# Decay products of a scan as two column halves, with the order of its neighbours changed, in a two-block transformer kernel

## The reference

```python
# stick-breaking attention, 8 heads
z = einsum('bqhd,bkhd->bhqk', q, k) * scale
log_keep = where(past, log_sigmoid(-z), 0.0)
between = cumsum(log_keep, axis=3, reverse=True) - log_keep
a = where(past, exp(log_sigmoid(z) + between), 0.0)
# even layer: short convolution, 3 taps, 1024 channels
y_a = sc_b * causal_depthwise_conv(sc_c * sc_v, sc_conv_w) * silu(sc_z)
# time steps of the scan, 32 heads
dt = softplus(ssd_dt + ssd_dt_bias)          # ssd_dt = h @ w_in[:, 9216:9248]
# scan, per chunk of 128 positions, 4 groups of 8 heads, 64 values a head
y_diag = einsum('bcqkg,bcqkgh,bckghp->bcqghp', cb, decay, xdt)
# output of the even layer: 3584 input channels
x = x + concat(y_b, y_mem, y_a) @ w_out
```

## Time and profile before

| | us |
|---|---|
| runs | 2659.9, 2661.48, 2664.15 |
| median | 2661.48 |
| the profiled execution | 2659.44 |
| its span | 2657.8 |
| TensorE busy in the span | 2635.8 (99%) |
| VectorE, ScalarE, GpSimd busy | 1564.2, 1343.3, 339.1 |

### The profile page before, as it was taken

The page is one execution under the profiler, slowest core; times in us unless marked ns, Lnnn a source line. Parts: engine busy times, 40 slices in busy tenths (PEclk is TensorE's granted clock), DMA queues, the critical chain, the costliest instruction groups (busy, mean ns, idle before and its releaser), DMA issues. The chain is left out here.

```text
span 2657.8 us, 35526 instructions
## 1 busy us (share of the span) xinstructions
PE 2635.8 (99%) x12007; PEld 2188.8 (82%) x12007; DVE 1564.2 (59%) x1833; ACT 1343.3 (51%) x1776; POOL 339.1 (13%) x523
## 2 busy tenths in 40 slices
PE   9999999999999999999999999999999999999998
PEld 7888888888888888888888888888888789888887
DVE  6444456667555555555455665446777765556864
ACT  6544455654444444444444554446565445554443
POOL 2100032211110000000000211001110110123400
PEclk9999999999999999999999999999999999999999
DMA  8876676678776767667666887667677777787775
GB/s 311 308 228 219 214 235 217 206 239 273 230 236 215 226 207 225 209 223 227 215 219 210 264 255 232 208 203 240 223 227 228 230 251 225 227 263 230 215 234 162
DMA packets 175720, 611.77 MB, mean 230 GB/s; under 512 B 23184, under 2 KB 26304, under 8 KB 175360
## 3 DMA queue, kind: packets, MB, share of 16 engines
q1 hardware_dynamic: 133632, 485.03, 56.2%
q0 software_dynamic: 37184, 121.07, 15.5%
q10 hardware_dynamic: 4800, 4.26, 0.6%
HBM read 559.36 MB, written 52.47 MB: 230 GB/s over the span
## 5 line engine op out<-in xcount | busy, mean ns | idle before, releaser
L1859 DVE TENSOR_TENSOR w_lo<-raw,w_hi 128x1024 fp32r<-128x1024 f32 x919 | 1116.4, 1222 | 865.2 <-ACT w_hi L1283 858.5
L1283 ACT ACTIVATE w_hi<-raw 128x1024 fp32r<-128x1024 f32 x919 | 963.9, 1058 | 914.7 <-PE acc L830 769.1
L824 PE MATMUL acc<-w_hi,x_t_hi 128*128 128x512 f32 (+1 forms) x2400 | 949.9, 396 | 0.4 <-ACT w_hi L1283 0.4
L824 PE MATMUL acc<-w_hi,x_t_lo 128*128 128x512 f32 (+1 forms) x2400 | 932.9, 389 | 0.0
L830 PE MATMUL acc<-w_lo,x_t_hi 128*128 128x512 f32 (+1 forms) x2400 | 639.9, 388 | 0.6 <-DVE w_lo L1859 0.6
L830 PEld LDWEIGHTS acc<-w_lo,x_t_hi 128*128 128x128 f32 x2400 | 450.5, 188 | 93.2 <-DVE w_lo L1859 1.0
L824 PEld LDWEIGHTS acc<-w_hi,x_t_hi 128*128 128x128 f32 x2400 | 450.9, 188 | 91.8 <-issue 1.9
L824 PEld LDWEIGHTS acc<-w_hi,x_t_lo 128*128 128x128 f32 x2400 | 451.0, 188 | 90.7 <-issue 1.9
L824 PE MATMUL acc<-w_hi,ff_t_hi 128*128 128x512 f32 x352 | 136.9, 389 | 0.0
L824 PE MATMUL acc<-w_hi,ff_t_lo 128*128 128x512 f32 x352 | 136.9, 389 | 0.0
L830 PE MATMUL acc<-w_lo,ff_t_hi 128*128 128x512 f32 x352 | 94.1, 389 | 0.0
(11 more groups left out here) (395 smaller groups left out, 2677.3 us busy)
## 6 DMA issues: line engine op xcount, KB each, us to landing
raw<-stream SPq DMA_DIRECT2D x919, 512.0 KB, 4.3
d_in<-tile POOLq DMA_DIRECT2D x20, 512.0 KB, 3.7
d_ev<-tile POOLq DMA_DIRECT2D x20, 512.0 KB, 4.9
d_x<-tile POOLq DMA_DIRECT2D x16, 512.0 KB, 4.4
r_b<-d_x POOLq DMA_DIRECT2D x64, 128.0 KB, 6.4
xin<-d_x POOLq DMA_DIRECT2D x16, 512.0 KB, 7.7
d_h<-tile POOLq DMA_DIRECT2D x14, 512.0 KB, 5.7
h_b<-d_h POOLq DMA_DIRECT2D x56, 128.0 KB, 4.6
```

The costliest lines, as they stand in the source:

```text
L824: nc.tensor.matmul(out, src[x][:, chunk + c, t * P:(t + 1) * P], w_hi[:, s, w], start=first and c == 0 and x == 0, stop=False)
L1283: nc.scalar.activation(w_hi[:, u.slot, :], raw[:, u.slot, :], ACT.Copy).then_inc(hi_ready, 1)
L1859: nc.vector.tensor_tensor(w_lo[:, s, :], raw[:, s, :], w_hi[:, s, :].bitcast(F32), ALU.subtract).then_inc(lo_ready, 1)
```

## The change

Six edits in one step.

- The decay products of the scan are issued as two halves of 64 stationary columns, at tile positions (0, 0) and (0, 64), each into its own half of the PSUM partitions.
- The time-step weights stand twice in their unit; VectorE turns the second copy into the low part (`split_beside`), so `w_hi` holds high and low parts side by side, 64 columns a chunk. TensorE makes 2 products a chunk. The two transposes become four fp32 products with pieces of the identity that add both halves.
- In the attention loop the third head's logarithm chain (`log_keep`) stands on ScalarE behind the split of position 7, ahead of the block's output.
- The first tap of the short convolution moves from VectorE to ScalarE (position 9j + 6), and the steps of VectorE are spread over positions 9j + 4 to 9j + 13, one a position; `sc_u` is transposed one position sooner, `sc_w` one later.
- EOUT_ORDER becomes units 0 to 9, 10 to 11 and 12 to 13 of blocks 0 and 1 in turn. TensorE waits for the halves at positions 20 and 24; block 0 ends at 25.
- The loop over the last "ein" units on VectorE is written out to place `split_beside`.

```diff
--- before.py
+++ after.py
@@ -32,7 +32,7 @@
 OLW = 448
 L_SCALE = 192 ** -0.5
 
-EOUT_ORDER = [(b, k) for ks in (range(10), range(10, 14)) for b in range(2) for k in ks]
+EOUT_ORDER = [(b, k) for ks in (range(10), range(10, 12), range(12, 14)) for b in range(2) for k in ks]
 TURN_AT = 3
 FIRST = [(b, k) for ks in (range(6), range(6, 8)) for b in range(2) for k in ks]
 FIRST_END = FIRST.index((0, 7))
@@ -201,7 +201,7 @@
         ("e_ac", [P, 32], F32), ("d_end", [P, 32], F32), ("g_ss", [P, 2], F32), ("g_ms", [P, 2], F32),
         ("g_r", [P, 2], F32), ("bm_t", [P, P], F32), ("cbm", [P, TH, P], F32),
         ("zt", [P, TH, NBW], F32), ("yb", [P, TH, NBW], F32))
-    dt_t = place("dt_t", [32, TOK], F32, XT + 10 * K)
+    dt_t = place("dt_t", [64, TOK], F32, XT + 10 * K)
     HG = 8
     SP_ = 64
     dec, u_in, cv, xs, xdt, xde, st = row_of(
@@ -1049,20 +1049,19 @@
         pe.wait_ge(lo_ready, u.times(1, 1 + RING))
         pe.wait_ge(m_lo, 5)
         for c in range(16):
-            w = slice(32 * c, 32 * c + P)
-            x_hi, x_lo = (x3_t[x][:, c, :] for x in range(2))
-            out = ps_y[:, 0:TOK]
-            nc.tensor.matmul(out, w_hi[:, u.slot, w], x_hi, start=c == 0, stop=False)
-            nc.tensor.matmul(out, w_lo[:, u.slot, w], x_hi, start=False, stop=False)
-            mm = nc.tensor.matmul(out, w_hi[:, u.slot, w], x_lo, start=False, stop=c == 15)
+            w = slice(64 * c, 64 * c + 64)
+            for x in range(2):
+                mm = nc.tensor.matmul(ps_y[0:64, 0:TOK], w_hi[:, u.slot, w], x3_t[x][:, c, :],
+                                      start=c == 0 and x == 0, stop=c == 15 and x == 1)
         mm.then_inc(unit_used, 1)
 
         def time_steps(p):
             if p == 1:
                 pe.wait_ge(dt_v, 1)
                 for t in range(TH):
-                    mm = nc.tensor.transpose(ps_y[:, TOK + 32 * t:TOK + 32 * t + 32], dt_t[:, t * P:(t + 1) * P],
-                                             ident[0:32, 0:32])
+                    for part in range(2):
+                        mm = nc.tensor.matmul(ps_y[:, TOK + 32 * t:TOK + 32 * t + 32], dt_t[:, t * P:(t + 1) * P],
+                                              ident[0:64, 32 * part:32 * part + 32], start=part == 0, stop=part == 1)
                 mm.then_inc(pe_once, 1)
             if p == 5:
 
@@ -1113,8 +1112,10 @@
                 for t in range(TH):
                     for h in range(HG):
                         w = slice(h * SP_, (h + 1) * SP_)
-                        nc.tensor.matmul(turn[t][:, w], dec[:, t, h * P:(h + 1) * P], xdt[:, t, w],
-                                         start=True, stop=True)
+                        for half in range(2):
+                            r = slice(half * SP_, (half + 1) * SP_)
+                            nc.tensor.matmul(turn[t][r, w], dec[:, t, h * P + half * SP_:h * P + (half + 1) * SP_],
+                                             xdt[:, t, w], start=True, stop=True, tile_position=(0, half * SP_))
                 pe.wait_ge(turn_lo, 2 * (TURN["sy"] + g) + 2)
                 nc.tensor.matmul(ps_y[:, :], cv[:, 5, P:TOK], st[:, :], start=True, stop=True).then_inc(s_y, 1)
 
@@ -1146,8 +1147,8 @@
             if q == 6:
                 pe.wait_ge(turn_lo, 2 * TURN["x4"] + 2)
                 pe.wait_ge(m_lo, 5)
-            if q in (20, 22):
-                pe.wait_ge(c_lo, q // 2 - 9)
+            if q in (20, 24):
+                pe.wait_ge(c_lo, q // 4 - 4)
             unit(At(U0["eout"] + q), z_t, UCH * k, (B0["eout"] + b) % 2, k == 0, k == 13)
         for b in range(2, 4):
             pe.wait_ge(sums_out, B0["eout"] + b + 1)
@@ -1393,17 +1394,20 @@
                 splits("win", 8, 8 * b, i, 16)
                 scale_out(At(U0["win"] + 8 * b + 7, i, 16), b, At(STORED["win"], i, 1).times(16, 16), 1)
 
+        def log_keep(j, i):
+            J, m = At(j, i, 4), At(j // 2, i, 2)
+            act.wait_ge(at_z, J.times(1, 2))
+            nc.scalar.activation(keep[:, :], z["sb"][:, :], ACT.Abs).then_inc(at_abs, 1)
+            act.wait_ge(at_abs, m.times(1, 1))
+            nc.scalar.activation(keep[:, :], keep[:, :], ACT.Exp, scale=-1.0).then_inc(at_exp0, 1)
+            act.wait_ge(at_exp0, m.times(1, 1))
+            nc.scalar.activation(keep[:, :], keep[:, :], ACT.Ln, bias=1.0).then_inc(at_keep, 1)
+
         def attend(p, i):
             for j in range(4):
                 J, m, s, kind = At(j, i, 4), At(j // 2, i, 2), j % 2, ("sb", "ca")[j % 2]
-                if p == HEAD_AT_UNIT[j] + 1 and kind == "sb":
-
-                    act.wait_ge(at_z, J.times(1, 2))
-                    nc.scalar.activation(keep[:, :], z["sb"][:, :], ACT.Abs).then_inc(at_abs, 1)
-                    act.wait_ge(at_abs, m.times(1, 1))
-                    nc.scalar.activation(keep[:, :], keep[:, :], ACT.Exp, scale=-1.0).then_inc(at_exp0, 1)
-                    act.wait_ge(at_exp0, m.times(1, 1))
-                    nc.scalar.activation(keep[:, :], keep[:, :], ACT.Ln, bias=1.0).then_inc(at_keep, 1)
+                if p == HEAD_AT_UNIT[j] + 1 and kind == "sb" and p != 7:
+                    log_keep(j, i)
                 if p == HEAD_AT_UNIT[j] + 2 and kind == "ca":
                     act.wait_ge(at_max, m.times(1, 1))
                     for x, w in enumerate((slice(0, P), slice(P, H3))):
@@ -1422,6 +1426,8 @@
         with act.Fori(0, 4) as i:
             for b in range(2):
                 splits("win", 8, 96 + 8 * b, i, 16, lambda k: attend(8 * b + k, i))
+                if b == 0:
+                    log_keep(HEAD_AT_UNIT.index(6), i)
                 scale_out(At(U0["win"] + 96 + 8 * b + 7, i, 16), b,
                           At(STORED["win"] + 6, i, 1).times(16, 16), 1)
 
@@ -1684,7 +1690,14 @@
             if k == 9 * j + 5:
                 act.wait_ge(c_u, j + 1)
                 nc.scalar.activation(sc_in[:, :, 2, :], sc_in[:, :, 3, :], ACT.Tanh, scale=0.5).then_inc(c_th, 1)
-            if k == 9 * j + 11:
+            if k == 9 * j + 6:
+                act.wait_ge(c_ut, j + 1)
+                act.wait_ge(c_y, j)
+                for c in range(4):
+                    at = 16 + 4 * j + c
+                    last = nc.scalar.activation(sc_cv[:, c, :], sc_u[:, c, :], ACT.Copy, scale=col2[:, at:at + 1])
+                last.then_inc(c_conv, 1)
+            if k == 9 * j + 12:
                 act.wait_ge(c_y, j + 1)
                 nc.scalar.activation(z_t[0][:, 20 + 4 * j:24 + 4 * j, :].rearrange("p c t -> p (c t)"),
                                      sc_y[:, :], ACT.Copy).then_inc(c_hi, 1)
@@ -1859,6 +1872,12 @@
             nc.vector.tensor_tensor(w_lo[:, s, :], raw[:, s, :], w_hi[:, s, :].bitcast(F32),
                                     ALU.subtract).then_inc(lo_ready, 1)
 
+        def split_beside(u):
+
+            dve.wait_ge(hi_ready, u.times(1, 1))
+            hi, src = (x[:, u.slot, :].rearrange("p (c h n) -> p c h n", h=2, n=32)[:, :, 1, :] for x in (w_hi, raw))
+            nc.vector.tensor_tensor(hi, src, hi.bitcast(F32), ALU.subtract).then_inc(lo_ready, 1)
+
         def splits(stage, units, first, i, per, hook=None):
             for k in range(units):
                 if hook:
@@ -2260,14 +2279,21 @@
                 turn_set(0)
             mem_job(0, At(0, i, 1), k - 6, z_t, At(16, i, 1).times(1))
 
-        for i in range(4):
+        for i in range(3):
             splits("ein", 16, 16, i, 16, lambda k: ein_beside(k, i))
+        for k in range(16):
+            ein_beside(k, 3)
+            u = At(U0["ein"] + 64 + k + LEAD)
+            if u.k == U0["dt"]:
+                split_beside(u)
+            else:
+                split(u)
         split(At(U0["dt"] + LEAD))
 
         def time_steps(p):
             if p == 0:
                 summed(At(U0["dt"]))
-                nc.vector.tensor_copy(dt_t[:, :], ps_y[0:32, 0:TOK]).then_inc(dt_v, 1)
+                nc.vector.tensor_copy(dt_t[:, :], ps_y[0:64, 0:TOK]).then_inc(dt_v, 1)
             if p == 2:
                 dve.wait_ge(pe_once, 2)
                 dve.wait_ge(cc, 3)
@@ -2409,48 +2435,48 @@
         for g in range(4):
             splits("sc", 16, 16 * g, 0, 0, lambda k: sc_beside(k, g))
 
+        def blocks_of(dst, part):
+            return nc.vector.transpose(dst[:, :, :].rearrange("p c (a i) -> p c a i", i=SQ),
+                                       sc_in[:, :, part, :].rearrange("p a (c i) -> p c a i", i=SQ))
+
         def short(k, j):
             if k == 9 * j + 4:
                 dve.wait_ge(c_in, 64 * (j + 1))
                 nc.vector.tensor_tensor(sc_in[:, :, 1, :], sc_in[:, :, 1, :], sc_in[:, :, 2, :], ALU.mult)\
                     .then_inc(c_u, 1)
+            if k == 9 * j + 5:
+                dve.wait_ge(c_u, j + 1)
+                dve.wait_ge(c_y, j)
+                blocks_of(sc_u, 1).then_inc(c_ut, 1)
             if k == 9 * j + 6:
                 dve.wait_ge(c_th, j + 1)
```

(36 more changed lines are left out.)

## The result

| | before | after |
|---|---|---|
| median, us | 2660.9 | 2645.4 |
| runs, us | 2659.9 to 2664.2 | 2642.5 to 2647.9 |
| profiled execution: span, us | 2657.8 | 2646.3 |
| ratio to before, 95% interval | 1 | 0.9937, 0.9924 to 0.9951 |

What follows compares the result with a forecast made beforehand. TensorE was taken as the bound, busy 2635.8 of 2657.8 us. Terms -4.1 - 4.8 + 3.0 - 1.1 + 1.7 = -5.3 us gave a median of 2656.2 us, range 2647.5 to 2666 us.

Steps and rivals of the forecast that it cites:

- logarithm: Attention loop: with the split ahead of the third head's logarithm, TensorE's wait for `p_t` goes, -4.1 us over 4 passes.
- waits in "eout": Short convolution's new steps and order: four TensorE waits worth 5.3 us go, 0.5 us left for raw weights, -4.8 us.
- later sum of block 0: Stage "eout": block 0 ends later, its store-and-load chain keeps its length, TensorE waits for the splits, +3.0 us (0.5 to 4).
- time steps: Time-step weights: 32 products instead of 48, -1.9 us, and four fp32 products for the transposes, +0.8 us; together -1.1 us.
- scan: Decay products: half records step at 0.057 us, tiles one after the other, plus 0.3 us tiling cost a group; +1.7 us.
- (a): Scan: the two column tiles run at once, 2.1 us a group, -5.7 us in place of +1.7, total 2648.8 us; chance 0.30.
- (b): Scan: a half's load takes as long as a whole one, 7.3 us a group, +15.3 us, total 2669.8 us; chance 0.13.
- (c): Scan: a step of 0.085 us from load and product order within a tile, +8.9 us, total 2663.4 us; chance 0.12.
- (d): Stage "eout": block 0's later end costs nothing because the chain shortens, total 2653.2 us; chance 0.42 together with the forecast.
- (e): Attention loop: reordering the logarithm does nothing, total 2660.3 us; chance 0.03.

Runs made afterwards that it cites:

- neighbours on one tile: Changed kernel with the loops around the scan's half products swapped, so neighbouring products share a column tile; 2650.9 us, ratio 0.9960 to the kernel before.
- whole products: Changed kernel with the scan's products undivided again, as before the change; 2651.4 us, ratio 0.9968 to the kernel before.
- four tiles: Changed kernel with each scan product in four column tiles of 32 output rows instead of two of 64; 2642.5 us, ratio 0.9938 to the kernel before.
- the version beyond: Changed kernel with block 0's transposes one unit later and one summed-identity product for the small time-step transposes; 2641.1 us, ratio 0.9930 to the kernel before.

## Why the prediction was wrong, point by point

| part | predicted, us | measured by the trace, us |
|---|---|---|
| logarithm | -4.1 | -4.1 (alone) |
| waits in "eout" | -4.8 | -5.3 |
| later sum of block 0 | +3.0 | +0.4 to +1.3, +0.7 in the changed kernel |
| time steps | -1.1 | -1.3 |
| scan | +1.7 | -5.5 |
| sum | -5.3 | -15.5 |

The four parts alone give ratios of 0.9982, 0.9988, 0.9984 and 0.9981, whose product is 0.9935, against 0.9937 for the whole change. They add up within their intervals, each some 2.5 us to either side; that the parts' sum by the trace and the difference of the medians are both 15.5 us is closer than either is known.

**A reading.** The prediction calls the wait for `p_t` the largest of TensorE's inside the kernel, and so does. The same view has one above it, line 830 waiting for `w_lo`, 3.3 us in 4 times. The sum does not suffer: the two of these four that lie in "eout" (2.4 us) are counted there, and the change does not touch the others.

**The scan: the step that failed.** "I take 0.057 us, load and stream both halved, tiles one after the other." The halves are right: with neighbours on one tile a record steps by 0.058 us. "One after the other" is wrong: two tiles give 0.029 and four 0.014. This one choice is 7.2 of the 10.2 us that I missed. It was rival (a), with 2.1 us a group forecast and (3.52 - 1.36) = 2.16 measured. I argued against it that "records start in order, and each product is two records on the same tile". The second half is true and no hindrance. The first does not hold from tile to tile, as far as the steps tell: split by tile, the changed kernel's starts put a product's two records 58 ns or more apart, with the other tile's record 6 to 7 ns behind each. Whether the engine changes the order or receives it so is not shown. The 0.3 us for going in and out of the tiling holds: 64 x 0.0295 + 0.3 = 2.19. Rivals (b) and (c) fall, since a half's record steps by 0.058 us on its own tile and not by 0.110 or 0.085.
By the Trainium skill, page TensorEngine Tiling (Array Packing), section Tiling Modes, different tiles can load and multiply in parallel; the traces agree, with 6 ns between the starts on two tiles and 58 ns between those on one. I had the rule before me and gave it 0.30 because no row of this kernel showed it. There was no row against it either, and the value that I took was itself no row's.

**The later sum of block 0: right mechanism, wrong size.** The pair of waits came where I said, for `w_lo` and then `w_hi`. The term failed at "Nothing in it gets shorter" and "16.36 us". The time from the store's issue to the transpose of block 0 in the twelve profiles:

| order | steps | chain, us |
|---|---|---|
| old | old (before, scan alone, time steps alone, logarithm alone) | 16.36, 15.82, 16.41, 14.70 |
| old | new (old order in the changed kernel) | 14.36 |
| new | old (order alone) | 13.39 |
| new | new (short convolution and order, after, neighbours on one tile, whole products, four tiles, the version beyond) | 14.32, 13.78, 13.57, 13.65, 14.00, 14.40 |

So the earlier trace rows showed the chain near its long end, and with both edits it is 1.9 us shorter in the mean (15.8 against 13.9). Either edit alone, in one profile each, has a chain as short as with both, so which of them shortens it isn't settled. For the changed kernel 3.0 - (16.36 - 13.78) = 0.4 us, against 0.7 measured. I had written "a microsecond or so" for this and then not taken it. Which transfer gets out of the chain's way was not tried and stays open. Rival (d), that the later sum costs nothing, was nearer than my term.

**The waits in "eout".** 5.3 us was the right size, and all of it goes; the 0.5 us that I left for raw weights was not needed. The mechanism holds: the raw weights are late by 8.66 us with the new order and old steps, and by 3.72 us at the most with the new steps (neighbours on one tile).

**Logarithm and time steps.** Both within 0.2 us, with the waits and record counts that I named. The eight small records step at 0.111 us against my 0.110. Rival (e), that the logarithm's new place does nothing, is out.

**The range.** It ended at 2647.5, which took in rival (a) with little of its spread (2648.8). Rivals (a) and (d) together would have been 2648.8 - 3.0 = 2645.8, within 0.4 us of the result. I treated them as alternatives, though they are independent, and never priced both coming true. That this sum comes so near is part luck: 0.7 us too little for the later sum and 0.7 us too few gained at the other waits and the time steps cancel.

## What to carry to other kernels

A product whose weight load sets its step (here 128 stationary columns against a stream of 64) gains from column tiles, as long as neighbours in the program lie on different tiles; the gain ends where the stream is the limit, at two tiles here. Before you take a duration of a chain of DMAs from one profile, look at the same chain at other places and in other profiles: in four kernels with the same code at this place it took from 14.70 to 16.41 us. And add independent rivals up when you set the ends of the range, for the best and the worst case are those in which several hold.

## What the runs showed of the hardware

The clock behind a wait. The wait of some 2.1 us for `w_lo` in "eout" occurs with the old steps in several profiles. The windows of the kernel with the new order alone:

```profile
2108.00:2111.00 3.00, 0.90 (x5) 1.00 0.00 0
2111.00:2113.00 2.00, 2.00 (x7) 0.58 0.79 262
2113.00:2115.00 2.00, 2.00 (x6) 0.56 0.67 242
2115.00:2120.00 5.00, 5.00 (x23) 1.00 0.84 256
```

TensorE stood still for 2.10 us, and then the records of 512 columns stepped at 0.427 us in place of 0.227 for about eight records, 1.6 us lost besides the wait. The kernels with the scan alone, the time steps alone and the logarithm alone show the same, while in the kernel before the same wait (2.12 us) was followed by a granted clock of 1.00. In the changed kernel the 2.7 us wait at 760 us has it too:

```profile
757.00:760.00 3.00, 0.37 (x2) 1.00 0.02 7
760.00:762.00 2.00, 1.53 (x5) 0.93 0.34 102
762.00:764.00 2.00, 2.00 (x6) 0.50 0.40 160
```

In all, nine waits in seven of the twelve profiles, 1.41 to 3.75 us long, were followed by a granted clock of 0.50. The 2.12 us of before and three waits of 1.50 to 1.81 us (one in the kernel with the scan alone, two in that with the order alone) were not, nor was the 2.9 us with which every profile starts. So the length of a wait doesn't decide it alone. Such a wait can cost near twice its length, and my price of a wait (its idle time and 0.27 us) was too low for these. The profile of before could not have told me.

The other thing is how cheap many small records are: 128 of them in 1.99 us, 0.014 us each, with their loads, as long as the tile changes from one to the next.
